# A top-k head in sixteen stripes in place of ten, and 80 candidate pairs in place of 256

## What is computed

```python
q = (xt @ w_q).reshape(n, 8, 2, 128)
s = einsum('nhpd,hpkd->nhpk', q, subkeys)            # 128 keys, two lists a head
s_top, i_top = lax.top_k(s, 16)
cand = s_top[:, :, 0, :, None] + s_top[:, :, 1, None, :]
best, sel = lax.top_k(cand.reshape(n, 8, 256), 16)
eidx = take_along_axis(i_top0 * 128 + i_top1, sel)   # 16 experts a head, 128 a token
gate = softmax(best)
a = gelu(u[eidx] . x);  out = sum(gate * a * v[eidx])
```

## Time and profile before

| | us |
|---|---|
| three runs | 4661.4, 4668.0, 4668.2 |
| median | 4668.0 |
| the profiled execution | 4653.4 |
| its span | 4651.9 |
| of it this stage | about 2023 to 3498 |

### The profile page before, as it was taken

How to read it: one execution, slowest core, us unless ns; L and a number is a source line. 1 busy time by engine, 2 the same in 40 slices (tenths; PEclk the granted TensorE clock), 3 DMA queues, 4 the chain that set the end, 5 groups by cost and what they waited for, 6 DMA issues and landing times. The chain is left out here.

```text
span 4651.9 us, 76801 instructions
## 1 busy us (share of the span) xinstructions
PE 4258.3 (92%) x28688; PEld 4148.1 (89%) x28688; DVE 2677.6 (58%) x3552; ACT 1249.7 (27%) x1625; POOL 1727.8 (37%) x1305
## 2 busy tenths in 40 slices
PE   5999999999698898979999988898886999999997
PEld 5999999999465798979999988888886999999997
DVE  4222112111322452246889999666666888888887
ACT  4111133332212221132323222222222333233232
POOL 0000000000111000002555545778785766766772
PEclk8999999999698999989999999999997999999998
DMA  4822333332476443135666656898887999999996
GB/s 159 312 81 82 126 111 105 107 111 86 142 261 254 139 136 122 63 135 195 240 233 232 219 198 241 322 340 314 323 309 292 373 355 363 357 359 358 359 354 259
DMA packets 279276, 1061.58 MB, mean 228 GB/s; under 512 B 43634, under 2 KB 94194, under 8 KB 225970
## 3 DMA queue, kind: packets, MB, share of 16 engines
q1 hardware_dynamic: 165490, 522.72, 31.9%
q0 software_dynamic: 93728, 510.53, 29.1%
q10 hardware_dynamic: 19936, 26.78, 1.6%
HBM read 977.47 MB, written 81.33 MB: 228 GB/s over the span
## 5 line engine op out<-in xcount | busy, mean ns | idle before, releaser
L139 DVE TENSOR_TENSOR w_lo<-w_raw,w_hi 128x1024 fp32r<-128x1024 f32 x498 | 599.6, 1228 | 1020.1 <-ACT w_hi L130 1010.2
L130 ACT ACTIVATE w_hi<-w_raw 128x1024 fp32r<-128x1024 f32 x498 | 518.9, 1058 | 1226.7 <-PE acc L167 756.5
L1307 POOL DMA_INDIRECT routes_scratch<-gate_sums,route x384 | 552.0, 1438 | 275.8 <-DVE gate_sums L1462 120.9
L167 PE MATMUL acc<-x_hi,w_hi 128*128 128x288 f32 x2592 | 552.3, 295 | 18.0 <-DVE w_lo L139 18.0
L167 PE MATMUL acc<-x_lo,w_hi 128*128 128x288 f32 x2592 | 551.5, 294 | 0.0
L167 PE MATMUL acc<-x_hi,w_lo 128*128 128x288 f32 x2592 | 551.2, 294 | 0.0
L167 PE MATMUL acc<-h_hi,w_hi 128*128 128x384 f32 (+1 forms) x1280 | 409.7, 336 | 85.6 <-DVE w_lo L139 85.4
L167 PE MATMUL acc<-h_hi,w_hi_peeru 128*128 128x384 f32 (+1 forms) x1280 | 409.4, 336 | 36.7 <-DVE w_lo_peeru L139 36.7
L167 PEld LDWEIGHTS acc<-x_hi,w_hi 128*128 128x128 f32 x2592 | 416.5, 189 | 18.7 <-DVE w_lo L139 15.1
L167 PEld LDWEIGHTS acc<-x_lo,w_hi 128*128 128x128 f32 x2592 | 416.7, 189 | 0.0
L167 PEld LDWEIGHTS acc<-x_hi,w_lo 128*128 128x128 f32 x2592 | 416.3, 189 | 0.0
(11 more groups left out here) (309 smaller groups left out, 8557.5 us busy)
## 6 DMA issues: line engine op xcount, KB each, us to landing
w_raw<-in_w_peer_u SPq DMA_DIRECT2D x256, 512.0 KB, 3.9
w_raw<-in_w_peer_v SPq DMA_DIRECT2D x256, 512.0 KB, 3.7
w_raw<-in_w_gate SPq DMA_DIRECT2D x96, 512.0 KB, 3.9
w_raw<-in_w_z SPq DMA_DIRECT2D x66, 512.0 KB, 3.3
k_ring<-in_cache_k SPq DMA_DIRECT2D x64, 512.0 KB, 5.1
v_ring<-in_cache_v POOLq DMA_DIRECT2D x64, 512.0 KB, 6.6
routes_scratch<-zero POOLq DMA_DIRECT2D x8, 3072.0 KB, 49.2
activations_scratch<-a_out ACTq DMA_DIRECT2D x128, 192.0 KB
```

Of the source, the lines that this page charges most:

```text
L130: nc.scalar.activation(slot(q, j)[0], raw[:, j % 4, :], ACT.Copy).then_inc(q["hi"], 1)
L139: nc.vector.tensor_tensor(lo, raw[:, j % 4, :], hi.bitcast(F32), ALU.subtract).then_inc(q["lo"], 1)
L167: last = nc.tensor.matmul(dst, l_, r_[:, cc, c0:c0 + cn], start=(cc == first and p_ == 0), stop=(cc == last_c and p_ == 2))
L1307: pool.indirect_dma_start(route_dram, bass.IndirectOffsetOnAxis(ap=route[:, b, n:n + 1], axis=0), gsum[:, h % SUMS, b - 1, n % PTOP:n % PT ...
```

## The change

GROUP is 16: a group holds two q stripes and fourteen u stripes, and after the eight groups 16 u stripes are left. A head's steps go over 17 stripes, one at a time: five `choose` of a block each in place of three, and the sums with earlier heads in three steps (`sums0` to `sums2`), each in its own stripe; an empty one does nothing. Head h is done in stripe 16h + 20 (head 0 in 12, as before), head 7 in 132. The dots: one a stripe from 16 to 38, then 1.5 a stripe to 134, then 2.5. The scatters: in each 24 gathers (one head) 4 before the first and three more before each next one, until the 48 of the head are issued; the last nine or so gathers have none between.

Of the 256 pairs only those are formed that can be among the best 16: the first of list one with all 16 of list two, the next seven with the first eight, and the last eight with the first one: 16 + 56 + 8 = 80. The position among these is unpacked otherwise: the second position by a mask (15, 7 or 0), the first by comparing the position with the start of each row (0, 16, 24, ... 64, 72 to 79; `first`) and summing the differences of neighbouring numbers (`steps_a`).

```diff
+        NCAND = 80
...
-        GROUP = 10
+        GROUP = 16
...
-        HEAD_STEPS = {4: ("list0",), 5: ("list1",), 6: ("list2",), 7: ("list3",), 8: ("list4",), 9: ("candidates", "choose0"),
-                      10: ("choose1",), 11: ("choose2", "shift"), 12: ("unpack", "look_up0"), 13: ("look_up1",), 14: ("number", "weigh"), 15: ("add_same",)}
-        FIRST_STEPS = {4: ("list0", "list1"), 5: ("list2", "list3"), 6: ("list4", "candidates"), 7: ("choose0",), 8: ("choose1",),
-                       9: ("choose2", "shift"), 10: ("unpack", "look_up0"), 11: ("look_up1", "number"), 12: ("weigh",)}
+        HEAD_STEPS = {4: ("list0",), 5: ("list1",), 6: ("list2",), 7: ("list3",), 8: ("list4",), 9: ("candidates",),
+                      10: ("choose0",), 11: ("choose1",), 12: ("choose2",), 13: ("choose3",), 14: ("choose4", "shift"), 15: ("unpack",),
+                      16: ("look_up0",), 17: ("look_up1", "number"), 18: ("weigh", "sums0"), 19: ("sums1",), 20: ("sums2",)}
+        FIRST_STEPS = {4: ("list0", "list1"), 5: ("list2", "list3"), 6: ("list4", "candidates"), 7: ("choose0", "choose1"),
+                       8: ("choose2", "choose3"), 9: ("choose4", "shift"), 10: ("unpack", "look_up0"), 11: ("look_up1", "number"), 12: ("weigh",)}
...
-        LAST_STEP = GROUP * (PH - 1) + 14
+        LAST_STEP = GROUP * (PH - 1) + 20
 
         def dots_by(s):
 
-            return 0 if s < 14 else min(NGAT, s - 13 if s < LAST_STEP else LAST_STEP - 13 + 2 * (s - LAST_STEP))
+            if s < 16:
+                return 0
+            return s - 15 if s <= 38 else min(NGAT, 23 + 3 * (min(s, 134) - 38) // 2 + 5 * max(0, s - 134) // 2)
 
         def scatters_before(q):
 
-            return 4 + 3 * q if q < 70 else min(NSCT, 214 + (q - 70) * 170 // 120)
+            return 48 * (q // 24) + min(48, 4 + 3 * (q % 24))
...
                 def candidates():
-                    link(nc.vector.tensor_tensor(cand[:].rearrange("p b (x y) -> p b x y", x=PTOP),
-                                                 top[:, :, 0, :].unsqueeze(3).to_broadcast([P, NBLK, PTOP, PTOP]),
-                                                 top[:, :, 1, :].unsqueeze(2).to_broadcast([P, NBLK, PTOP, PTOP]), ALU.add))
-
-                def choose(blocks):
-                    link(sixteen([(cand[:, b, :], rest_c[:, n, :], best[:, b, :], sel[:, b, :]) for n, b in enumerate(blocks)]))
+
+                    one, two = top[:, :, 0, :], top[:, :, 1, :]
+                    nc.vector.tensor_tensor(cand[:, :, 0:16], one[:, :, 0:1].to_broadcast([P, NBLK, 16]), two, ALU.add)
+                    nc.vector.tensor_tensor(cand[:, :, 16:72].rearrange("p b (x y) -> p b x y", x=7), one[:, :, 1:8].unsqueeze(3).to_broadcast([P, NBLK, 7, 8]),
+                                            two[:, :, 0:8].unsqueeze(2).to_broadcast([P, NBLK, 7, 8]), ALU.add)
+                    link(nc.vector.tensor_tensor(cand[:, :, 72:80], one[:, :, 8:16], two[:, :, 0:1].to_broadcast([P, NBLK, 8]), ALU.add))
+
+                def choose(b):
+                    link(sixteen([(cand[:, b, :], rest_c[:, b % 2, :], best[:, b, :], sel[:, b, :])]))
...
                 def unpack(h):
                     dve.wait_ge(s_lst, NBLK * (h + 1))
-                    nc.vector.tensor_scalar(sel_a[:, 0], sel[:], 4, None, ALU.logical_shift_right)
-                    link(nc.vector.tensor_scalar(sel_a[:, 1], sel[:], PTOP - 1, None, ALU.bitwise_and))
+                    nc.vector.tensor_scalar(wide[:], sel[:], 16.0, 8.0, ALU.is_lt, ALU.mult)
                     nc.vector.tensor_copy(tidx_f[:], tidx[:])
-                    link(nc.vector.tensor_copy(sel_f[:], sel_a[:]))
+                    nc.vector.tensor_copy(sel_f[:, 0], sel[:])
+                    link(nc.vector.tensor_scalar(used[:], sel[:], 72.0, None, ALU.is_lt))
+                    link(nc.vector.scalar_tensor_tensor(out=mask_b[:], in0=wide[:], scalar=7.0, in1=used[:], op0=ALU.add, op1=ALU.mult))
+                    nc.vector.tensor_copy(steps_a[:, :, 0:1], tidx_f[:, :, 0, 0:1])
+                    nc.vector.tensor_tensor(steps_a[:, :, 1:PTOP], tidx_f[:, :, 0, 1:PTOP], tidx_f[:, :, 0, 0:PTOP - 1], ALU.subtract)
+                    link(nc.vector.tensor_tensor(sel_b[:], sel[:], mask_b[:], ALU.bitwise_and))
+                    link(nc.vector.tensor_copy(sel_f[:, 1], sel_b[:]))
...
-                def add_same(h):
-
-                    dve.wait_ge(s_lst, NBLK * (h + 1) + (h < PH - 1))
-                    for h0 in range(0, h, 3):
+                def add_same(h, part_no):
+
+                    h0 = 3 * part_no
+                    if h0 == 0 and h < PH - 1:
+                        dve.wait_ge(s_lst, NBLK * (h + 1))
+                    if h0 < h:
...
+                    if part_no == 2:
+                        dve.sem_inc(s_head, 1)
```

More of the change, by code:

```diff
@@ L1197, in build @@
         tidx_f = then("tidx_f", [P, NBLK, 2, PTOP], F32)
-        sel_a = then("sel_a", [P, 2, NBLK, PTOP], U32)
+        sel_b = then("sel_b", [P, NBLK, PTOP], U32)
+        mask_b = then("mask_b", [P, NBLK, PTOP], U32)
         sel_f = then("sel_f", [P, 2, NBLK, PTOP], F32)
@@ L1209, in build @@
         best = then("best", [P, NBLK, PTOP], F32)
+        first = then("first_of_row", [P, PTOP], F32)
+        wide, used = (then(x, [P, NBLK, PTOP], F32) for x in ("mask_wide", "mask_used"))
+        steps_a = then("first_list_steps", [P, NBLK, PTOP], F32)
         sel = then("sel", [P, NBLK, PTOP], U32)
@@ L1215, in build @@
         qp = then("qp", [P, 2, NBLK * P], F32)
-        cand = then("cand", [P, NBLK, PTOP * PTOP], F32)
+        cand = at("cand", [P, NBLK, NCAND], F32, place[0])
+        place[0] += NBLK * PTOP * PTOP * 4
         rest_l = at("rest_of_lists", [P, 2, 2, NKEY], F32, place[0])
-        rest_c = at("rest_of_candidates", [P, 2, PTOP * PTOP], F32, place[0])
+        rest_c = at("rest_of_candidates", [P, 2, NCAND], F32, place[0])
         onehot = then("onehot", [P, NBLK, PTOP, PTOP], F32)
@@ L1252, in build @@
         exp_at = {s + 1: h for s in plan for h, name in plan[s] if name == "shift"}
-        move_at = {s + 1: h for s in plan for h, name in plan[s] if name == ("add_same" if h else "weigh")}
-        LAST_STEP = GROUP * (PH - 1) + 14
+        move_at = {s + 1: h for s in plan for h, name in plan[s] if name == ("sums2" if h else "weigh")}
+        LAST_STEP = GROUP * (PH - 1) + 20
         def dots_by(s):
-            return 0 if s < 14 else min(NGAT, s - 13 if s < LAST_STEP else LAST_STEP - 13 + 2 * (s - LAST_STEP))
+            if s < 16:
+                return 0
+            return s - 15 if s <= 38 else min(NGAT, 23 + 3 * (min(s, 134) - 38) // 2 + 5 * max(0, s - 134) // 2)
         def scatters_before(q):
-            return 4 + 3 * q if q < 70 else min(NSCT, 214 + (q - 70) * 170 // 120)
+            return 48 * (q // 24) + min(48, 4 + 3 * (q % 24))
         with nc.Block() as block:
@@ L1441, in look_up @@
                     link(nc.vector.tensor_tensor(flat, sel_f[:, side].rearrange("p b k -> p (b k)").unsqueeze(2).to_broadcast([P, NBLK * PTOP, PTOP]),
-                                                 iota[:].unsqueeze(1).to_broadcast([P, NBLK * PTOP, PTOP]), ALU.is_equal))
-                    link(nc.vector.tensor_tensor(onehot[:], onehot[:], tidx_f[:, :, side, :].unsqueeze(2).to_broadcast([P, NBLK, PTOP, PTOP]), ALU.mult))
+                                                 (iota if side else first)[:].unsqueeze(1).to_broadcast([P, NBLK * PTOP, PTOP]),
+                                                 ALU.is_equal if side else ALU.is_ge))
+                    link(nc.vector.tensor_tensor(onehot[:], onehot[:], (tidx_f[:, :, 1, :] if side else steps_a[:]).unsqueeze(2).to_broadcast([P, NBLK, PTOP, PTOP]), ALU.mult))
                     link(nc.vector.reduce_sum(part[:, side].rearrange("p b k -> p (b k)"), flat, AX.X))
@@ L1466, in weigh @@
                         link(last)
-                def add_same(h):
-                    dve.wait_ge(s_lst, NBLK * (h + 1) + (h < PH - 1))
-                    for h0 in range(0, h, 3):
+                def add_same(h, part_no):
[3 more added lines that the diff above has]
+                    if h0 < h:
+                        if part_no == 2 and h < PH - 1:
+                            dve.wait_ge(s_lst, NBLK * (h + 1) + 1)
                         n = min(3, h - h0) * PTOP
@@ L1478, in add_same @@
                         link(nc.vector.reduce_sum(psum_[:], same[:, :, :, 0:n], AX.X))
[L1479 to L1482, removed]
+                        link(nc.vector.tensor_tensor(gsum[:, h % SUMS], gsum[:, h % SUMS], psum_[:], ALU.add))
+                    if part_no == 2:
+                        dve.sem_inc(s_head, 1)
                 def step(h, name):
@@ L1489, in step @@
                     elif name.startswith("choose"):
-                        choose(((0, 1), (2, 3), (4,))[int(name[6:])])
+                        choose(int(name[6:]))
                     elif name == "shift":
@@ L1501, in step @@
```

(5 more changed lines are left out.)

## The result

The changed kernel takes 4676.0 us (median of 12 runs) against 4664.4 of the kernel before beside it (12 runs): a ratio of **1.0023, 95% interval 1.0012 to 1.0033, 0.2% slower**. Forecast were 49 us less and a range of 4567 to 4668.

What follows compares the result with a forecast made beforehand. POOL, issuing gathers and scatters and held by VectorE, was taken to end the chain; sums 21, middle 32 and end 162 put the stage's end at 3449, not 3497.7: 48.7 us less, 4619 us, range 4567 to 4668.

Steps and rivals of the forecast that it cites:

- What bounds the kernel now: Stage over w_peer_q and w_peer_u: 150 us above its floor; POOL, issuing gathers and scatters in one order, ends the chain.
- The hold: On POOL: an indirect DMA is held until the VectorE operation running at its start has ended; started free it takes 0.98.
- The floor of 1286: Stage from first to last drain if TensorE never stalls: 1286 us, where 1436.5 were measured before.
- Part 1, candidates: Choosing on VectorE: 80 candidates for 256 take VectorE from 1135 to about 1102 us; alone this ends no wait.
- Part 2, the sums: Stripes with heads 3 to 7's sums: VectorE falls behind, 21 us lost; 7 more from the clock left to the range.
- Part 3, the middle: Bursts of three scatters a gather at 6.7 us on POOL: 5.4 us lost a head, 32 for six heads.
- The formula 11c - 64 - 4: Per head's burst: lateness of the twelfth gather's dot, c being three scatters and a gather, less 4 covered; 5.4 us lost.
- Part 4, the end: After stripe 131, head 7's remaining gathers and scatters with c = 6.8: 162 us, stage ending at 3449, not 3497.7.
- rival C: POOL finds a VectorE operation running at every start: c 8.8, stage ends near 3620, 4790 us; chance 0.09.
- Rival D: VectorE is held by POOL too, 197 us more on VectorE, about 4670 us; chance 0.03.
- Rival B: POOL is hardly held: c near 5.1, stage ends at 3391, 4561 us; chance 0.19 with half-way cases.
- Signs: Expected in the trace: no stall to about stripe 45, POOL waiting hardly, then long, each head; some 60 us w_lo stalls after head 7.

Runs made afterwards that it cites:

- run 1: The changed kernel with two scatters in place of three between gathers; 4588.1 us, ratio 0.9838 to the kernel before.
- run 3: The changed kernel with each dot made a sum over the gathered row alone, one SBUF input; one execution, stage 1335.5 us.
- run 9: The changed kernel with groups of fourteen, two scatters a gather, head 7's sums apart, 1.5 dots a stripe from stripe 25; 4544.2 us, ratio 0.9751 to before.
- run 4: The kernel before with the 80 candidates alone, its groups of ten, dots and scatters kept; ratio 1.0007 to the kernel before.
- run 2: The changed kernel without the 384 scatters and the waits for them; one execution, stage 1318.2 us against the changed kernel's 1462.3.
- run 10: The changed kernel with two scatters a gather and all 256 candidates; ratio 0.9876 to the kernel before.

## Why the prediction was wrong

*What bounds the kernel now* held: POOL issuing, and held by VectorE; runs 1 and 3 show both. The hold as the forecast words it, by whatever runs on VectorE, is too wide: the searches (69 transfers) and run 3's sums over one input (175) held none. The floor of 1286 held too: run 9 comes within 22 us of it.

*Part 1, candidates*: right. 237 ns a search, VectorE 37 us less by run 4 (forecast 33), no wait ended there.

*Part 2, the sums* (21): 27 are lost at their places, 9 of them by the lower clock, the third that I had left to the range. That it comes so near is luck. Without scatters (run 2) all stripes up to 131 lose 9, 8.4 of it at stripe 131, so the sums' own price is nearer 9. The rest is VectorE coming late out of a burst: before the stall of stripe 129, counted here, it waits 3.4 us for a row and then has head 7's look-up.

*Part 3, the middle* (32): **this step failed; it measured 81.** The price c of three scatters and a gather was 7.2 to 7.3 us in the fourteen full cycles of each burst of heads 2 to 6, not 6.7. (Head 1's mean is 7.6, with 8.9 us of waits for dots in it.) Never held, a cycle takes 5.1. The forecast's 6.7 left 1.6 for the hold, the late rows of before have 1.7, and these bursts have 2.1 to 2.2. In head 4's fourteen cycles 15 transfers are held behind dots, 19.6 us together, and 10 behind splits, 10.0: 1.4 and 0.7 a gather, where the late rows have 1.2 and 0.5. There were 0.7 pairs of splits to a dot now and 0.5 then, and the early rows, where POOL idled beside the dots, pulled the mean further down.

The formula 11c - 64 - 4 gives 12 a head and 74 in all at the measured c. It prices waiting alone, and there it is too high: in these 81 us TensorE is idle for 56. The other 25 are matmuls at the lower clock level behind each stall, a term that the forecast named for the sums and left out here. So two errors of the step stand beside the wrong c and nearly cancel.

I had written that nothing is gained from c = 7.3 on and given that 0.14 in all, 0.09 for slower and 0.05 for no change. With 7.3 in the middle and 6.85 at the end, the forecast's sum has the stage 6 us shorter than before. It was 14 longer, so the wrong c takes the gain away and doesn't by itself give the sign.

*Part 4, the end* (162 from stripe 131): 169.8. c was 6.85 there, 6.8 taken. Six of the eight stand ahead of head 7's first gather, 27 behind that drain and not 21. Right, with a size a little off.

*The forecast as a sum*: the stage was to end 1399 us after its first drain and ends after 1462. Of the 63, 49 are the middle, 6 the sums, 8 the end.

The prediction's *rival C* (slower) is what happened in direction, but not at its price: of the 56 transfers of a burst's fourteen cycles 27 were held, not all. *Rival D* is excluded by the dots' unchanged pace: 129 dots with POOL busy beside them for over 80% of their time last 2.27 to 2.33 us, 58 without it 2.29. *Rival B*'s world is that of run 3: POOL less held, 5.8 to 6.0 a cycle, and a stage 127 us shorter.

*Signs*: the first stall near stripe 45, POOL without waits in bursts and idle behind them (171.6 us), TensorE stalling behind head 7: all seen. They would have been seen at c = 6.7 too. They tell the mechanism and not the sign.

*The ratio*: before, the late stretch had cost 105 and the sums 45; now 60 at the end, 81 in bursts and 27 at the sums. The change took away part of what it aimed at and paid it back through an order of scatters that packs a head's 48 into fifteen gathers.

## What to carry to other kernels

When two streams share a queue, price the ratio in which they stand in each stretch, at the mean that this mixture would have beside that stretch's other work, not at a mean from a stretch with another mixture. If the sum changes sign within the spread of one such price, say so in the chances. A burst of side work on an issuing queue costs more than the same work spread evenly, even where the queue is idle a fifth of the time; here one digit in the order of the scatters was worth 84 us. Work saved on an engine is worth little in stretches where another engine is what is waited for: the 80 candidates were worth nothing in run 4 and next to nothing in run 10. And a stall of TensorE has two prices: here 121 us stood idle and 47 went to a lower clock behind the stalls.

## What the runs showed of the hardware

An indirect DMA on POOL, scatter or gather, takes 0.97 us in these traces. Started while VectorE ran an operation on two inputs in SBUF (a dot, a split, a product or comparison of 1280 or 2304 elements) it ended 0.92 to 0.95 behind that operation in the rows shown, and 0.85 (median) behind its recorded end in all. A 2048-element reduction of the same 2.28 us with one input didn't hold it, nor did the searches: in two stretches (2724 to 2832, 2887 to 2995) the scatters of run 3 had means of 1.08 and 1.13 against 1.42 and 1.48. VectorE shows no delay from POOL (2.29 us a dot with and without it). I had not expected how steady that makes POOL's rate: in the bursts of heads 2 to 6 the mean was 7.2 to 7.3 us a gather, with no wait but this one.
